# Recurrent stage: the squarings of the chunk inverse by pairs of chunks, on 64x64 tiles of TensorE

## What is computed

```python
def wkv7_scan(r, w, k, v, a, b, reverse):
    def step(state, inp):
        r_t, w_t, k_t, v_t, a_t, b_t = inp
        sa = jnp.einsum('bhvk,bhk->bhv', state, a_t)
        state = state * w_t[:, :, None, :] + sa[..., None] * b_t[:, :, None, :] + v_t[..., None] * k_t[:, :, None, :]
        return state, jnp.einsum('bhvk,bhk->bhv', state, r_t)
```

## Time and profile before

| what | value |
|---|---|
| median of 3 executions | 2813.72 us (2809.47 to 2813.91) |
| the profiled execution's own time | 2813.53 us |
| its span in the profile | 2811.4 us |
| mean granted clock of TensorE | 0.963 of 2.4 GHz |
| busy: PE, DVE, ACT | 2541.8, 1192.9, 751.5 us |
| recurrent stage, the eight groups | 1354 to 1608 us of the span |
| experts, from the router on | 1844 us to the end |

### The profile page before, as it was taken

The page is one execution under the profiler, slowest core; times in us unless marked ns, Lnnn a source line. Parts: engine busy times, 40 slices in busy tenths (PEclk is TensorE's granted clock), DMA queues, the critical chain, the costliest instruction groups (busy, mean ns, idle before and its releaser), DMA issues. The chain is left out here.

```text
span 2811.4 us, 52284 instructions
## 1 busy us (share of the span) xinstructions
PE 2541.8 (90%) x22984; PEld 1782.8 (63%) x22984; DVE 1192.9 (42%) x2004; ACT 751.5 (27%) x1211; POOL 59.7 (2%) x52
## 2 busy tenths in 40 slices
PE   7998889899999999899888879979988999889887
PEld 7998667799999988677666656743333333333222
DVE  7764766544466642666432357631111111111113
ACT  3221454442344321444222126421000000000001
POOL 1000022000000000000000000010000000000000
PEclk9999999999999999999899899999999999999999
DMA  5545441455322233433213112579999999999996
GB/s 162 140 126 123 104 152 58 137 174 165 115 97 98 87 102 110 153 112 116 84 47 102 41 68 73 190 297 430 430 430 431 430 431 430 431 431 429 431 431 275
DMA packets 142785, 609.71 MB, mean 217 GB/s; under 512 B 37664, under 2 KB 57248, under 8 KB 117536
## 3 DMA queue, kind: packets, MB, share of 16 engines
q1 hardware_dynamic: 113616, 570.97, 52.4%
q10 hardware_dynamic: 28944, 35.40, 3.9%
HBM read 566.50 MB, written 37.47 MB: 215 GB/s over the span
## 5 line engine op out<-in xcount | busy, mean ns | idle before, releaser
L3811 PE MATMUL moe_bank<-moe_ring,xg 128*64 128x512 f32 x2048 | 490.6, 623 | 87.9 <-DMA moe_ring<-in_w_exp_up 87.2
L3811 PEld LDWEIGHTS moe_bank<-moe_ring,xg 128*64 128x64 f32 x2048 | 154.6, 142 | 366.5 <-issue 357.8
L4096 DVE TENSOR_TENSOR moe_sg<-moe_sg,moe_bank 64x512 f32<-64x512 f32 x64 | 44.1, 690 | 576.4 <-ACT moe_sg L3963 576.4
L3840 PE MATMUL moe_bank<-moe_ring,moe_act_t 128*64 128x512 f32 x1008 | 227.0, 592 | 0.5 <-ACT moe_act_t L3970 0.5
L68 PE MATMUL ffn_prod<-ffn_x_low,ffn_w_high 128*128 128x258 f32 x704 | 200.2, 284 | 5.8 <-PEq L138 5.8
L69 PE MATMUL ffn_prod<-ffn_x_high,ffn_w_low 128*128 128x258 f32 x704 | 200.1, 284 | 0.0
L70 PE MATMUL ffn_prod<-ffn_x_high,ffn_w_high 128*128 128x258 f32 x704 | 199.3, 283 | 0.0
L68 PE MATMUL in_bank<-x_low,in_w_high 128*128 128x264 f32 x640 | 185.0, 289 | 15.6 <-DVE in_w_low L987 10.4
L70 PE MATMUL in_bank<-x_high,in_w_high 128*128 128x264 f32 x640 | 183.2, 286 | 0.0
L69 PE MATMUL in_bank<-x_high,in_w_low 128*128 128x264 f32 x640 | 182.7, 286 | 0.0
L3840 PEld LDWEIGHTS moe_bank<-moe_ring,moe_act_t 128*64 128x64 f32 x1008 | 72.2, 137 | 144.0 <-issue 143.4
(11 more groups left out here) (589 smaller groups left out, 5230.9 us busy)
## 6 DMA issues: line engine op xcount, KB each, us to landing
moe_ring<-in_w_exp_gate SPq DMA_DIRECT2D x64, 2048.0 KB, 27.6
moe_ring<-in_w_exp_up SPq DMA_DIRECT2D x64, 2048.0 KB, 21.3
moe_ring<-in_w_exp_down SPq DMA_DIRECT2D x63, 2048.0 KB, 25.8
ffn_w<-in_w_up SPq DMA_DIRECT2D x44, 512.0 KB, 4.4
in_w<-in_w_in SPq DMA_DIRECT2D x40, 512.0 KB, 4.2
front_w<-in_w_in SPq DMA_DIRECT2D x32, 512.0 KB, 3.5
ffn_w<-in_w_down SPq DMA_DIRECT2D x16, 704.0 KB, 4.1
rw_w<-in_w_in SPq DMA_DIRECT2D x18, 512.0 KB, 4.2
```

Of the source, the lines that this page charges most:

```text
L3811: last = nc.tensor.matmul(bank[64 * g:64 * g + 64, s], xe[:, (e // BATCH) % 2, k, at:at + CAPACITY], ring[:, slot_of(n, g), k * HALF:(k + ...
L3840: last = nc.tensor.matmul(bank[64 * h:64 * h + 64, 3 + e % 2], act_t[:, s, j], weights[:, at:at + HALF], start=(c == 0 and j == 0), stop=( ...
L4096: nc.vector.tensor_tensor(sg[0:CAPACITY, s], sg[0:CAPACITY, s], bank[64:64 + CAPACITY, s], ALU.mult).then_inc(act_ready, 1)
```

## The change

Two chunks are taken together. A pair's two triangles lie on the diagonal of a 64x64 matrix whose other blocks are zero, and one product with a 64x64 tile takes the place of two with 32x32 tiles. For that each head has seven blocks of 32 columns in place of three: A with the odd chunks zeroed, A with the even chunks zeroed, A; the same three of AT; and the product. The zeros are made by multiplying with 0 and 1: in `mask` by wider masks, between the rounds by `sides`, three column blocks in `eyes`. `ch` loses its buffer per group, the finished inverse gets a buffer of its own (`inv`), and two buffers of the memory's sums move into `states`.

```diff
-        masks = sb("masks", [P, 2, 5, RCHUNK])
-        eyes = sb("eyes", [P, HEAD_DIM + RCHUNK])
+        masks = sb("masks", [P, 2, 9, RCHUNK])
+        eyes = sb("eyes", [P, HEAD_DIM + 4 * RCHUNK])
...
-        ch = sb("ch", [P, 2, 2, heads_all, 3 * RCHUNK])
+        ch = sb("ch", [P, 2, heads_all, 7 * RCHUNK])
+        inv = sb("inv", [P, heads_all, RCHUNK])
...
                 def powers(g, l):
                     act.wait_ge(round_made, LEVELS * g + l + 1)
-                    nc.scalar.copy(ch[:, g % 2, (l + 1) % 2, :, A], bank[:, CHAIN_BANK + 1, 0:heads_all * RCHUNK].rearrange(
-                        "p (n f) -> p n f", f=RCHUNK)).then_inc(power_ready, 1)
+                    made = bank[:, CHAIN_BANK + 1, 0:heads_all * RCHUNK].rearrange("p (n f) -> p n f", f=RCHUNK)
+                    for q in range(3 if l + 1 < LEVELS - 1 else 2):
+                        last = nc.scalar.activation(ch[:, (l + 1) % 2, :, q * RCHUNK:(q + 1) * RCHUNK], made, ACT.Copy,
+                                                    scale=sides[:, q, 0:1])
+                    last.then_inc(power_ready, 1)
...
                     for n in range(heads_all):
                         at = 2 * RCHUNK * n
-                        for c in range(4):
-                            last = nc.tensor.matmul(bank[rows(c), CHAIN_BANK, at + first:at + upto], now[rows(c), n, A],
-                                                    now[rows(c), n, first:upto], start=True, stop=True)
+                        for c in range(2):
+                            last = nc.tensor.matmul(bank[heads(c), CHAIN_BANK, at + first:at + upto], now[heads(c), n, A_BOTH],
+                                                    now[heads(c), n, AT_ONE.start + first:AT_ONE.start + upto], start=True, stop=True)
                         if l < LEVELS - 1:
-                            for c in range(4):
-                                last = nc.tensor.matmul(bank[rows(c), CHAIN_BANK + 1, n * RCHUNK:(n + 1) * RCHUNK], now[rows(c), n, AT],
-                                                        now[rows(c), n, A], start=True, stop=True)
+                            for c in range(2):
+                                last = nc.tensor.matmul(bank[heads(c), CHAIN_BANK + 1, n * RCHUNK:(n + 1) * RCHUNK],
+                                                        now[heads(c), n, AT_BOTH], now[heads(c), n, A_ONE], start=True, stop=True)
...
-                        first = ch[:, g % 2, 0, e::2].rearrange("p x (q f) -> p x q f", q=3)
-                        nc.vector.tensor_tensor(first[:, :, 0:3:2], made[:, :, 0:5:4], masks[:, d, 0:5:4].unsqueeze(1).broadcast_to(
-                            [P, RW_X, 2, RCHUNK]), ALU.mult).then_inc(masked, 1)
+                        first = ch[:, 0, e::2, 0:6 * RCHUNK].rearrange("p x (a q f) -> p x a q f", a=2, q=3)
+                        for a, n in ((0, 4), (1, 0)):
+                            nc.vector.tensor_tensor(first[:, :, a], made[:, :, n].unsqueeze(2).broadcast_to([P, RW_X, 3, RCHUNK]),
+                                                    masks[:, d, 3 * a + 3:3 * a + 6].unsqueeze(1).broadcast_to([P, RW_X, 3, RCHUNK]),
+                                                    ALU.mult).then_inc(masked, 1)
...
                     if l < LEVELS - 2:
-                        nc.vector.tensor_copy(ch[:, g % 2, (l + 1) % 2, :, AT], made[..., AT]).then_inc(inverse_ready, 1)
+                        three = [P, heads_all, 3, RCHUNK]
+                        nc.vector.tensor_tensor(ch[:, (l + 1) % 2, :, AT_PLACE].rearrange("p n (q f) -> p n q f", q=3),
+                                                made[..., AT].unsqueeze(2).broadcast_to(three),
+                                                sides.unsqueeze(1).broadcast_to(three), ALU.mult).then_inc(inverse_ready, 1)
...
```

More of the change, by code:

```diff
@@ L2728, in rwkv7 @@
         eye_head = eyes[:, 0:HEAD_DIM]
-        eye_chunk = eyes[:, HEAD_DIM:]
+        eye_chunk = eyes[:, HEAD_DIM:HEAD_DIM + RCHUNK]
+        sides = eyes[:, HEAD_DIM + RCHUNK:].rearrange("p (q f) -> p q f", q=3)
+        first_states = states[:].rearrange("p a n k -> p (a n k)")
+        mem_sums = first_states[:, 0:2 * TM].rearrange("p (j t) -> p j t", j=2)
+        mem_scale = first_states[:, 2 * TM:3 * TM]
         TURN_BANK = (2, 5, 2)
@@ L2737, in rwkv7 @@
         GATE_BANK = (7, 2, 3)
-        AT, PT, A = (slice(n * RCHUNK, (n + 1) * RCHUNK) for n in range(3))
+        AT, PT = (slice(n * RCHUNK, (n + 1) * RCHUNK) for n in range(2))
+        A_BOTH, A_ONE = slice(0, 2 * RCHUNK), slice(2 * RCHUNK, 3 * RCHUNK)
+        AT_BOTH, AT_PLACE = slice(3 * RCHUNK, 5 * RCHUNK), slice(3 * RCHUNK, 6 * RCHUNK)
+        AT_ONE, P_PLACE = slice(5 * RCHUNK, 6 * RCHUNK), slice(6 * RCHUNK, 7 * RCHUNK)
         B_TOK, K_TOK, V_TOK = (slice(n * FIELD, n * FIELD + HEAD_DIM) for n in range(3))
@@ L3070, in chain_round @@
                 def chain_round(g, l):
-                    now = ch[:, g % 2, l % 2]
+                    now = ch[:, l % 2]
                     if l == 0:
-                        pe.wait_ge(masked, 4 * (g + 1))
+                        pe.wait_ge(masked, 6 * (g + 1))
                         if g >= 1:
@@ L3234, in finish_side @@
                         dve.wait_ge(mem_scale_ready, 2)
-                        nc.vector.tensor_tensor(out[:, s, 0:TM], bank[:, s, 0:TM], mem_scale[:], ALU.mult).then_inc(out_ready, 1)
+                        nc.vector.tensor_tensor(out[:, s, 0:TM], bank[:, s, 0:TM], mem_scale, ALU.mult).then_inc(out_ready, 1)
                     else:
@@ L3294, in inverse @@
                     dve.wait_ge(inverse_ready, INVERSES[-1] * g + INVERSES[l])
-                    nc.vector.tensor_tensor(ch[:, g % 2, (l + 1) % 2, :, PT], ch[:, g % 2, l % 2, :, PT], made[..., PT],
-                                            ALU.add).then_inc(inverse_ready, 1)
+                    to = ch[:, (l + 1) % 2, :, P_PLACE] if l < LEVELS - 1 else inv[:]
+                    nc.vector.tensor_tensor(to, ch[:, l % 2, :, P_PLACE], made[..., PT], ALU.add).then_inc(inverse_ready, 1)
                 def read_ends(g):
@@ L4384, in laid_out @@
     d["ident"] = np.eye(P, dtype=f32)
-    d["rw_eyes"] = np.concatenate([np.tile(np.eye(n, dtype=f32), (P // n, 1)) for n in (HEAD_DIM, RCHUNK)], 1)
+    d["rw_eyes"] = np.concatenate([np.tile(np.eye(n, dtype=f32), (P // n, 1)) for n in (HEAD_DIM, RCHUNK)] + [
+        np.repeat((n // RCHUNK % 2 == side).astype(f32)[:, None], RCHUNK, 1) for side in range(2)] + [
+        np.ones((P, RCHUNK), f32)], 1)
     d["slots"] = np.broadcast_to(np.arange(1, CAPACITY + 1, dtype=f32), (P, CAPACITY))
@@ L4391, in laid_out @@
     s, t = n[:, None] % RCHUNK, np.arange(RCHUNK)[None, :]
-    d["rw_masks"] = np.stack([np.stack([s < t, s <= t, s < t, s <= t, s > t], 1),
-                              np.stack([s > t, s >= t, s > t, s >= t, s < t], 1)], 1).astype(f32)
+    sides = [(n // RCHUNK % 2 == side)[:, None] for side in range(2)] + [np.ones((P, 1), bool)]
+    d["rw_masks"] = np.stack([np.stack([a <= b, a < b, a <= b] + [(a > b) & side for side in sides] +
+                                       [(a < b) & side for side in sides], 1) for a, b in ((s, t), (t, s))], 1).astype(f32)
     return {name: np.ascontiguousarray(a) for name, a in d.items()}
```

21 lines of the change are left out of this document (10 added, 11 removed).

## The result

The changed kernel took **2791.57 us** (median of 4 runs, 2778.24 to 2800.12) against 2813.81 (4 runs, 2809.47 to 2817.81): a ratio of 0.9913, 95% interval 0.9892 to 0.9935, which is 0.7 to 1.1% faster. Run again on another chip it gave 2791.02 against 2818.32, ratio 0.9901 (0.9886 to 0.9915). The forecast was 2800.2, range 2782 to 2820, "faster" with 0.68. The profiled execution took 2792.68 us.

The account below looks back on a forecast made before the run. The prediction took the recurrent stage as bound by PE's instruction supply as much as by its products. From 2813.53 us, 17.7 - 23.5 - 10.3 + 1 + 1.8 = -13.3 gave 2800.2 us, range 2782 to 2820.

Parts of the forecast that it names:

- columns: PE's rounds in the eight groups: 64x64 passes take 61 ns each, 7.09 us a group, adding 17.7 us.
- issue waits: PE's stalls for instructions in the eight groups: fewer records, so 40.5 us fall to 17, -23.5 us.
- clock: PE's granted clock over the eight groups rises from 0.93 to about 0.97, giving back 10.3 us.
- waits between rounds for DVE and ACT: Longer copies between rounds exceed the cover of 256-wide side products by 0.3 us in three groups, +1 us.
- the stage's start: Before the first round, larger masks take longer to load and make: 0.7 plus 1.1 us, +1.8 us.
- rival (d): Weight loads hide in the rounds: a pass stays at 49 ns, -31 us, 2782.5 us; chance 0.06.
- 1.1 us a place, 17 us in all: Stalls left at 15 dense steps (`finish_ends`, `scores`), averaged over where packets' ends can fall.
- Packets: Instruction packets in the eight groups: 60 fall to 46.3, each holding 4.9 us of PE work.
- the clock follows the stalls in the same share: Clock loss in the eight groups shrinks like the stalls: 23.5 / 40.5 of 17.8 us, -10.3 us.
- rival (c): DVE's longer copy bounds PE between rounds, 0.4 us in three rounds of eight groups: -4, 2809.5 us; chance 0.09.
- Rival (a): Ends, scores and rows keep their stalls, 32 us stay: +8.3, 2821.8 us; chance 0.14.
- Rival (b): PE's stalls have another cause than instruction supply, so nothing is given back: 2834 us; chance 0.04.

Follow-up runs that it names:

- moved by a quarter: Changed kernel plus 16 idle 32x32 products before the stage's first round, shifting later instruction packets' ends by a quarter packet: 2797.96 us, 0.9942 of the kernel before.
- by a half: Changed kernel plus 32 idle 32x32 products before the stage's first round, shifting later instruction packets' ends by half a packet: 2795.09 us, 0.9936 of the kernel before.
- the records back in each head: Changed kernel with as many unread 4-column products behind each head's pairs as the change removed: 2871.73 us, 1.0192 of the kernel before.

## Why the prediction was right

The mechanism held in the main, and two of its sizes did not; by its terms, in us, over the stage:

| term | forecast | measured |
|---|---|---|
| columns: rounds at full clock, 0.95 + 1.18 + 1.18 + 0.95 + 0.55 = 4.81 a group to 4 x 1.52 + 0.81 = 6.89, times 8 | +17.7 | +16.6 |
| issue waits, 40.0 to 6.9 | -23.5 | -33.1 |
| clock, (1 - 0.93) x 254 = 17.8 to (1 - 0.95) x 229 = 11.5 | -10.3 | -6.3 |
| waits between rounds for DVE and ACT, (3.4 - 2.3) + 0.3 | +1 | +1.4 |
| the stage's start | +1.8 | +2.2 |
| sum | -13.3 | -19.2 |

Measured as lengths, the start grew by 2.2 and the eight groups shrank by 24.5: -22.3. The 3.1 us between that and the sum of the terms are not assigned. Stages ahead of this one took 1.9 us more and those behind 0.2 less in this execution, which makes the span's -20.6.

*Columns*: right. A pass takes (1388.64 - 1387.12) / 24 = 63 ns with its entry, (1388.43 - 1387.26) / 20 = 58 without; the choice of the state steps' 61 over the 49 of then was the right one, and rival (d), whose loads hide, falls. The forecast's 0.62 and 0.89 us for a last round take in the end of its last product, the 0.55 and 0.81 above do not; the difference is the same but for 0.01.

*Supply*: right in kind, and **the mis-sized step is "1.1 us a place, 17 us in all"** for the dense steps: the stalls left are 6.9 us. One part of the error is the placement: moved ends give 9.3 and 15.4, so the mean over placements is nearer 10.5 than 17, and the kernel as written drew the good end of it. The other part is a second kind of stall. Three of the seven waits left (1.08, 1.73 and 1.72 us, 4.5 of the 6.9) stand at the end of packets that hold 3.8 to 4.9 us of work; by the forecast's count PE should not have stalled there. It did, since the next packet came late. Here is one, from the end of the wait at L70 to the end of that at L3067, and below it the packet that ended in the longest stall of the kernel before:

```profile
1489.74:1495.78 6.04, 4.31 (x128) 3.30 (x129) 0.35 (x1) 0.59 (x1) 0.00 (x0) 1.00 0.62 252
```
```profile
1485.63:1491.95 6.32, 2.41 (x128) 1.84 (x127) 0.00 (x0) 0.48 (x1) 0.00 (x0) 1.00 1.05 408
```

Each has the 127 to 129 records of a packet of the earlier trace rows, but took 6.04 and 6.32 us where those took 3.30 to 3.98, and the DMA engines were moving 252 and 408 GB/s (114 and 4 in the two rows shown in the earlier trace rows). The trace has each packet's own transfer too: it began 3.58 and 3.68 us behind the end of the wait before, in the six of the earlier trace rows 1.05 to 1.36; and in every run an issue wait ended 2.2 to 3.0 us behind the beginning of such a transfer. So the dense steps, 17 us in the forecast, left about 2.4 here, and late packets, at which it put nothing, 4.5. That it is the other transfers which delay the packets is read from their coming together; no run moved them by themselves.

*Packets*: 46.3 forecast, 45 came; 4.9 us of work in one, measured 4.8.

*Clock*: **"the clock follows the stalls in the same share" failed**: 0.95 came, not the 0.97 looked for. Before, nine stretches at 1.2 GHz lay in the stage, 37.5 us: two of 6.8 us each, by the two waits of PE for DVE (the start; group 1, round 2), and seven of 3.4 us, each by a wait with no engine named; one of these is the earlier trace rows. After, the seven became one (the last of the three windows above), which alone gives back 20.5 / 2 = 10.2 us, the forecast's number. But the two that go with DVE's waits are still there and grew, to 7.9 (counted from the first round on) and 13.65 us, though the wait in group 1 is the same (2.34 and 2.39 us): 4.0 us of work lost anew. In the repeated run these two are there with the same lengths and the seven are all gone. The wait alone doesn't set the length: the wait in group 1 is 2.36 and 2.37 us with the packets' ends moved by a quarter and by a half, and 3.4 us at 1.2 GHz go with it in the one and none in the other. What else does stays open.

*DVE and ACT*: right. DVE is named before two rounds and ACT before one; rival (c), with DVE in front of every round, falls.

*The start*: right in size. In the repeated run the wait for DVE is 2.88 us in place of 3.85, but there an issue wait of 1.05 us stands just ahead of it, in `scores`: together they are as long.

*The sum and the chances*: the time fell near the forecast partly by luck. The supply gave 9.6 us more and the clock 4.0 less than forecast, and the place of the packets' ends decides over much of the first: moved by a quarter, the groups shrink by 16.8 us and not by 24.5. Nine tenths of the forecast and (d), 0.67 + 0.06, are 0.66, not the 0.68 given for "faster"; nothing else hangs on it.

Rival (a), dense steps that keep their stalls, would have needed over 26 us of issue waits; the worst placement has 15.4. Rival (b), another cause, is told apart by the experiments: with everything of the change but the pairs the time is 0.9993 of before, and with the pairs the stalls go as far as the records do. The Trainium skill ("Runtime: NRT & Kernel Launch", section "Instruction fetch mechanics"), which calls a crossing of 256 instructions "mostly hidden", is right for the changed stage (6.9 of 229 us) and wrong for the stage before (40.0 of 253): the runs show it hidden as far as the work of a packet exceeds its refill, which was 3.30 to 3.98 us in the earlier trace rows and over 6 in the two packets above.

No run beat the changed kernel by more than its interval.

## What to carry to other kernels

Where the waits of an engine name no other engine, count its records between the ends of two stalls and set the work of such a batch against the refill's time: here 3.5 us of work against 3.7 cost 40 us in 253. Then fewer and larger products win even where each one is slower for the array: PE got 16.6 us more of work in the rounds and the stage got 24.5 us shorter. A gain of this kind depends on where the batches end (6.9 to 15.4 us of stalls for the same stage), so a small edit upstream can move it by some 8 us, 0.3% of this kernel. And look at the transfers under way at each stall: two refills that met a busy DMA took over 6 us here, and 4.3 us of work did not cover one of them.

## What the runs showed of the hardware

- A round of 64x64 tiles doesn't get shorter when its columns halve from 64 to 32 in one of the two products: 1.52 us both. The tile of 64 rows with 4 columns of weights and 4 moving takes at most 28 ns. That points to the weight load; since both counts changed, the runs don't separate them.
- A change of the tile's shape between neighbouring products cost about 0.1 us (0.21 against 0.12 from one product to the next, in the rows at 1501): twice in a head it made 48 tiny records dearer than the round's own products.
- The clock can fall without a wait of PE ahead of it. With the records back in each head, PE was busy in 7.24 of the 7.40 us before a fall (its one wait there is 0.17 us; before another fall, at 1596.5, it was busy in all of 7.40), and then ran at the lower level for 17 us, busy in 16.85 of them (windows of that kernel):

```profile
1432.00:1439.40 7.40, 7.24 (x252) 6.25 (x252) 3.48 (x7) 2.81 (x7) 0.00 (x0) 1.00 0.13 32
1439.50:1456.50 17.00, 16.85 (x325) 14.50 (x325) 2.41 (x6) 3.90 (x10) 0.00 (x0) 0.50 0.10 36
```

  In the stretch before the fall shown it ran a round with tiny products between the pairs, `finish_ends` and side products. That kernel lost 0.13 of its clock over the stage (0.87), with 4.2 us of issue waits.
